# Low part of the weights in two halves on GpSimd, and the per-head sums of squares as two fp32r matmuls

## The reference, cut to what matters

```python
def rmsnorm(x, g):
    x32 = x.astype(jnp.float32)
    y = x32 * lax.rsqrt(jnp.mean(x32 * x32, axis=-1, keepdims=True) + EPS)
    return (y * g.astype(jnp.float32)).astype(x.dtype)

p = h @ w_in[l]
xr, yr, q, k, v, ga, gb = jnp.split(p, cuts, axis=-1)
q = head_rmsnorm(q.reshape(b_, s_, ATT_HEADS, HEAD_DIM), q_norm_g[l])
k = head_rmsnorm(k.reshape(b_, s_, ATT_HEADS, HEAD_DIM), k_norm_g[l])
y_b = stick_breaking_attention(q, k, v)
mix = jax.nn.sigmoid(ga) * y_a + jax.nn.sigmoid(gb) * y_b
x = x + gt1 * (mix @ w_out[l])
```

## Time and profile before

| what | us |
|---|---|
| median of 3 runs (lowest, highest) | 1753.96 (1753.73, 1754.41) |
| time of the profiled execution | 1748.95 |
| its span, first to last instruction | 1747.1 |
| PE busy | 1664.6 (95%) |
| DVE busy | 1020.6 (58%) |
| ACT busy | 789.6 (45%) |
| POOL busy | 711.2 (41%), of which L595 641.7 (532.1 and 109.6) |

### The profile page before, as it was taken

The page is one execution under the profiler, slowest core; times in us unless marked ns, Lnnn a source line. Parts: engine busy times, 40 slices in busy tenths (PEclk is TensorE's granted clock), DMA queues, the critical chain, the costliest instruction groups (busy, mean ns, idle before and its releaser), DMA issues.

```text
span 1747.1 us, 19411 instructions
## 1 busy us (share of the span) xinstructions
PE 1664.6 (95%) x7340; PEld 1346.0 (77%) x7340; DVE 1020.6 (58%) x1156; ACT 789.6 (45%) x986; POOL 711.2 (41%) x325
## 2 busy tenths in 40 slices
PE   3999999999889999999999999999999999999997
PEld 2777787777668878878877888777778877887875
DVE  6676778677637927825632767566437474255642
ACT  2555556565434414523342333676544444244442
POOL 1233333342354444444444543454464151542524
PEclk7999999999899999999999999999999999999999
DMA  9333333332232332233322322211123131331312
GB/s 359 133 109 121 121 123 109 112 106 95 66 96 85 96 95 95 91 118 97 97 73 90 106 90 75 70 41 55 48 85 98 48 109 37 109 97 37 109 48 73
DMA packets 46460, 166.87 MB, mean 96 GB/s; under 512 B 5152, under 2 KB 5280, under 8 KB 45856
## 3 DMA queue, kind: packets, MB, share of 16 engines
q1 hardware_dynamic: 46368, 165.63, 29.1%
HBM read 163.52 MB, written 2.10 MB: 95 GB/s over the span
## 4 chain that ended last, share of the span: by engine, by line
PE 85%; DVE 10%; ACT 2%; issue 1%; DMA 1%; POOL 1%; SPq 0%; DVEq 0%; ACTq 0%
PE lin L621 16%; PE lin L623 16%; PE lin L622 16%; PE big L621 6%; PE big L622 6%; PE big L623 6%; DVE scr L1510 1%; DVE scr L1784 1%; PE m_a L657 1%; PE m_o L740 1%; PE big L720 1%; DVE tmp L2089 1%; DVE y_hi L1793 1%; PE big L731 1%; PE big L733 1%
## 5 line engine op out<-in xcount | busy, mean ns | idle before, releaser
L595 POOL TENSOR_TENSOR w_lo<-raw,w_hi 128x1024 fp32r<-128x1024 f32 (+1 forms) x215 | 532.1, 2480 | 741.3 <-ACT w_hi L1053 740.7
L621 PE MATMUL lin<-h_hi,w_hi 128*128 128x512 f32 x952 | 380.6, 400 | 4.7 <-POOL w_lo L595 3.6
L623 PE MATMUL lin<-h_hi,w_lo 128*128 128x512 f32 x952 | 371.1, 390 | 0.0
L622 PE MATMUL lin<-h_lo,w_hi 128*128 128x512 f32 x952 | 370.8, 389 | 0.0
L1053 ACT ACTIVATE w_hi<-raw 128x1024 fp32r<-128x1024 f32 (+1 forms) x215 | 223.9, 1041 | 160.8 <-PE m_b L639 49.2
L621 PEld LDWEIGHTS lin<-h_hi,w_hi 128*128 128x128 f32 x952 | 179.1, 188 | 46.8 <-POOL w_lo L595 6.6
L622 PEld LDWEIGHTS lin<-h_lo,w_hi 128*128 128x128 f32 x952 | 179.0, 188 | 39.9 <-issue 4.1
L623 PEld LDWEIGHTS lin<-h_hi,w_lo 128*128 128x128 f32 x952 | 178.8, 188 | 37.8
L595 POOL TENSOR_TENSOR qk_hl<-raw,qk_hl 128x1024 fp32r<-128x1024 f32 (+1 forms) x44 | 109.6, 2493 | 159.8 <-ACT qk_hl L1053 159.8
L621 PE MATMUL lin<-y_hi,w_hi 128*128 128x512 f32 x324 | 128.7, 397 | 12.0 <-DVE y_lo L1671 6.9
L622 PE MATMUL lin<-y_lo,w_hi 128*128 128x512 f32 x324 | 127.2, 393 | 0.0
(11 more groups left out here) (440 smaller groups left out, 3199.5 us busy)
## 6 DMA issues: line engine op xcount, KB each, us to landing
raw<-weights SPq DMA_DIRECT2D x245, 512.0 KB, 3.6
slab<-ada SPq DMA_DIRECT2D x32, 512.0 KB, 4.3
scr<-ada SPq DMA_DIRECT2D x16, 512.0 KB, 6.3
raw<-weights SPq DMA_DIRECT2D x10, 256.0 KB, 2.8
x<-x_t SPq DMA_DIRECT2D x2, 1024.0 KB, 6.1
out_t<-scr SPq DMA_DIRECT2D x8, 256.0 KB, 2.1
raw<-weights SPq DMA_DIRECT2D x4, 448.0 KB, 3.4
rgw<-rg_w SPq DMA_DIRECT2D x1, 1024.0 KB, 6.5
```

What stands on the lines that cost most here:

```text
L595: nc.gpsimd.tensor_tensor(lo[:, 0:w], raw[:, s, 0:w], hi[:, 0:w].bitcast(F32), ALU.subtract).then_inc(w_split, 1)
L621: nc.tensor.matmul(psum_of(n), wh, hi(k), start=(k == 0), stop=False)
L622: nc.tensor.matmul(psum_of(n), wh, lo(k), start=False, stop=False)
L623: last = nc.tensor.matmul(psum_of(n), wl, hi(k), start=False, stop=(k == nk - 1))
```

## The change: what it does

**Halves on POOL.** For an entry wider than 512 columns POOL makes the low part in two subtractions, the first of 512 columns, the second of the rest. The first raises a new semaphore `w_half`, which nobody waits for; the second raises `w_split` as before.

**Sums of squares in fp32r.** For the 16 sums of the heads' loop ACT writes the square to `sq_act` as before, then copies it as the high part in fp32r to `sq_hi` (for queries the tile `y_hi[:, 6]`, for keys the tail of `cq_hi`); DVE subtracts it and stores the low part in `sq_lo`; PE multiplies high and low by the full block of ones of `sel_r`, two fp32r matmuls in the place of one in float32. The other sums of squares stay as they were.

```diff
@@ gpsimd, for each entry e
                 pool.wait_ge(w_high, e + 1)
-                nc.gpsimd.tensor_tensor(lo[:, 0:w], raw[:, s, 0:w], hi[:, 0:w].bitcast(F32),
+                if w > 4 * P:
+                    nc.gpsimd.tensor_tensor(lo[:, 0:4 * P], raw[:, s, 0:4 * P], hi[:, 0:4 * P].bitcast(F32),
+                                            ALU.subtract).then_inc(w_half, 1)
+                at = 4 * P if w > 4 * P else 0
+                nc.gpsimd.tensor_tensor(lo[:, at:w], raw[:, s, at:w], hi[:, at:w].bitcast(F32),
                                         ALU.subtract).then_inc(w_split, 1)
@@ tensor
+            def head_square(i, out=m_a[:]):
+                pe.wait_ge(sq_low, i)
+                nc.tensor.matmul(out, sel_r[:, 1], sq_hi[(i - 1) % 2], start=True, stop=False)
+                nc.tensor.matmul(out, sel_r[:, 1], sq_lo[(i - 1) % 2], start=False, stop=True)\
+                    .then_inc(square_used, 1)
...
-                    square(8 + 2 * h + 1, True, True)
+                    head_square(2 * h + 1)
...
-                    square(8 + 2 * h + 2, True, True)
+                    head_square(2 * h + 2)
@@ scalar
+            def head_square(i, src):
+                full = sq_act[:, i % 2]
+                if i > 2:
+                    act.wait_ge(sq_low, i - 2)
+                nc.scalar.activation(full, src, ACT.Square).then_inc(sq_full, 1)
+                act.wait_ge(sq_full, counted(sq_full))
+                if i > 2:
+                    act.wait_ge(square_used, DK + i - 2)
+                nc.scalar.activation(sq_hi[(i - 1) % 2], full, ACT.Copy).then_inc(sq_high, 1)
+                act.wait_ge(sq_high, counted(sq_high))
...
-                    square(9 + 2 * h, A(S1["q"], h))
+                    head_square(2 * h + 1, A(S1["q"], h))
...
-                    square(10 + 2 * h, A(S1["k"], h))
+                    head_square(2 * h + 2, A(S1["k"], h))
@@ vector
+            def square_low(i):
+                dve.wait_ge(sq_high, i)
+                v.tensor_tensor(sq_lo[(i - 1) % 2], sq_act[:, i % 2], sq_hi[(i - 1) % 2].bitcast(F32), SU)\
+                    .then_inc(sq_low, 1)
+                dve.wait_ge(sq_low, counted(sq_low))
             for h in range(HEADS):
                 g = h - 1
+                square_low(2 * h + 1)
                 if g >= 0:
                     dve.wait_ge(z_done, g + 1)
                     dve.wait_ge(ln_done, g + 1)
                     shifted_logs()
+                square_low(2 * h + 2)
                 if h < HEADS:
                     accumulate(ADA_FIRST + 4 * h)
```

More of the change, by code:

```diff
@@ L216, in build @@
         w_high = sem("w_high")
+        w_half = sem("w_half")
         w_split = sem("w_split")
@@ L257, in build @@
         mixed = sem("mixed")
+        sq_full = sem("sq_full")
+        sq_high = sem("sq_high")
+        sq_low = sem("sq_low")
         rooted = sem("rooted")
@@ L486, in build @@
         lm_lo = cq_lo[:].rearrange("p a t -> p (a t)")[:, 0:1280]
+        sq_hi = [y_hi[:, 6], cq_hi[:].rearrange("p a t -> p (a t)")[:, 1280:1280 + T]]
+        sq_lo = [y_lo[:, 6], cq_lo[:].rearrange("p a t -> p (a t)")[:, 1280:1280 + T]]
         block = ctx.enter_context(nc.Block())
@@ L654, in square @@
             def square(count, first, last, out=m_a[:]):
-                pe.wait_ge(squared, count)
+                pe.wait_ge(squared, count if count <= DK else count - 2 * HEADS)
                 nc.tensor.matmul(out, c_("ones"), sq_act[:, count % 2], start=first, stop=last)\
+                    .then_inc(square_used, 1)
[3 more added lines that the diff above has]
+                nc.tensor.matmul(out, sel_r[:, 1], sq_lo[(i - 1) % 2], start=False, stop=True)\
                     .then_inc(square_used, 1)
@@ L772, in _ @@
                 if h == 0:
-                    square(8 + 2, True, True, m_b[:])
+                    head_square(2, m_b[:])
                 elif h < HEADS:
                     pe.wait_ge(rooted, 2 * h + 1)
-                    square(8 + 2 * h + 2, True, True)
+                    head_square(2 * h + 2)
                 if g >= 0:
```

## The result

| what | before | after |
|---|---|---|
| median (lowest, highest), us | 1753.95 (1753.73, 1754.41), 4 runs | 1734.01 (1732.94, 1735.07), 4 runs |
| profiled execution, its span | 1748.95, 1747.1 | 1733.2, 1731.3 |
| mean granted clock of the profiled execution | 0.986 | 0.986 |

The ratio is 0.9886, with a 95% interval of 0.9869 to 0.9903. The change gains 19.9 us by the medians, and 15.75 us by the two profiled executions. The forecast was 8.9 us and 1745.1, with a range that ended at 1740.5. So the direction was right and the size wrong by more than a factor of two.

What follows compares the result with a forecast made beforehand. PE was taken as the bound, busy for 310.00 of 310 us in turns h = 2 to 7. Sums of squares 6.4 us plus halves 2.45 make 8.9; 1753.96 - 8.9 = 1745.1 us, range 1740.5 to 1751.

Steps and rivals of the forecast that it cites:

- part two: Halves on POOL, over the whole run: shorter holds of DVE gain 4.05 us, later entry ends lose 1.6, net 2.45.
- 6.4 + 2.45: Whole run: 6.4 us from the heads' loop's cheaper sums of squares plus 2.45 from the halves on POOL, 8.9 us.
- The first waits for one half and the second for the other, and the sum is as before: Where two held DVE instructions follow each other, each waits for one half, so halving an entry gains nothing.
- the two other waits behind L1795 [...]: nothing: Two PE waits behind a held cast and a plain subtraction: the second half holds the subtraction, so no gain.
- At 430.28 [...] 1.0 us gained: At 430.28 us one DVE block, L1510, is held with PE's modulation behind it; a half gains 1.0 us.
- up to 2 us more where a shifted start lets DVE go first: Upper bound of the halves' gain: DVE starts ahead of POOL and doesn't wait, up to 2 us more.
- The list of places: PE's waits behind DVE's low parts, the modulation block and POOL's low parts: all that the halves can change.
- The slack behind `lm_done`: Heads' loop: a delay of 1 to 2 us from DVE's first new subtraction is covered by 4.6 us.
- the wait of 1.99: PE's wait for `lm_done` in h = 1: 0.40 us less work becomes 0.40 us more waiting, one saving lost.
- I take the same difference off that: The profiled execution stands 5.0 us below the median, before and after alike, so the median becomes 1745.1.
- more than 12, by shifted holds: Case for the whole run: a gain of more than 12 us, by shifted holds; chance 0.03.
- 1751.5: Rival's time if a new PE wait eats all the sums' saving: within 0.4 of no change; within 3.5, chance 0.12.

Runs made afterwards that it cites:

- e1: The kernel before with only the halves on POOL added, sums of squares still in float32: 1743.72 us, ratio 0.9943.
- e2: The kernel before with only the fp32r sums of squares added, POOL's entries whole: 1749.19 us, ratio 0.9974.
- e6: The changed kernel with halves only for entries ahead of w_out, whole entries from there on: 1743.85 us, ratio 0.9948 to the kernel before.
- e7: The changed kernel with whole entries ahead of w_out, halves only from there on: 1740.86 us, ratio 0.9936 to the kernel before.
- e8: The changed kernel with whole entries on POOL and sums from the squares' high part alone, one fp32r matmul: 1744.13 us, ratio 0.9951 to the kernel before.

## Why the prediction was wrong, step by step

The step that failed first is the price of part two, "4.05 - 1.6 = 2.45 us": the halves alone bring 7.0 us at one clock (e1). The second is that the two parts were added as if they didn't touch, 6.4 + 2.45: together they bring 16.0, some 5 more than e1 and e2 apart. The third is the step from the profiled execution to the median, which misses another 4. The mechanism, that POOL's instruction holds DVE's and that a half holds it half as long, was right.

**The sums were right.** Each saves 0.41 us (forecast 0.40 and 0.45). No wait for `sq_low` came, and the two engines' additions in the turns were covered.

**"The first waits for one half and the second for the other, and the sum is as before" was used where it doesn't hold; "the two other waits behind L1795 [...]: nothing" failed at the first of them.** I looked only at the two DVE instructions right ahead of PE. What starts them counts as well. This is the place at 615 us. ACT and DVE there in before:

```profile
609.13 0.63 ACT L1266 ACTIVATE scr<-scr 128x512 f32<-128x512 f32 x1 [1.58 <-DVE scr L1784]
```
```profile
600.66 2.82 DVE L1795 TENSOR_TENSOR y_lo<-tmp,y_hi 128x512 fp32r<-128x512 f32 x1
603.51 2.50 DVE L1757 TENSOR_SCALAR tmp<-tmp 128x512 f32<-128x512 f32 x1
...
607.50 3.10 DVE L1784 SCALAR_TENSOR_TENSOR scr<-big,par,scr 128x511 f32<-128x511 f32 x4
...
611.37 2.45 DVE L1793 CAST y_hi<-tmp 128x512 fp32r<-128x512 f32 x1
```

and after:

```profile
596.98 0.63 ACT L1295 ACTIVATE scr<-scr 128x512 f32<-128x512 f32 x1
```
```profile
594.91 1.53 DVE L1822 SCALAR_TENSOR_TENSOR scr<-big,par,scr 128x511 f32<-128x511 f32 x2
...
599.35 1.40 DVE L1831 CAST y_hi<-tmp 128x512 fp32r<-128x512 f32 x1
600.78 1.63 DVE L1833 TENSOR_TENSOR y_lo<-tmp,y_hi 128x512 fp32r<-128x512 f32 x1
```

The cast and the subtraction do behave as I said: 2.45 and 0.69 became 1.40 and 1.63. But ACT had sat idle for 1.58 us ahead of its Gelu (L1266), until DVE's convolution was done, since two DVE instructions ahead of that (L1795 and L1757 above) had been held for 2.1 us each; with halves the Gelu starts right behind ACT's own work. That is the 1.5 us. The runs bear it out: with whole entries there PE waits 2.9 us at this place (e2, e6), with halves 1.64 (e1, e7 and the change). At the third such wait, 880 us in before, PE's idle time fell only from 1.79 to 1.64 us, as good as forecast.

**"At 430.28 [...] 1.0 us gained" took the hold as halved; in the whole change it went.** POOL and DVE there, after:

```profile
423.31 2.00 POOL L602 TENSOR_TENSOR w_lo<-raw,w_hi 128x512 fp32r<-128x512 f32 x1 [3.64 <-ACT w_hi L1070]
...
422.90 1.29 DVE L1539 SCALAR_TENSOR_TENSOR scr<-slab,par,scr 128x1024 f32<-128x1024 f32 x1
```

In before POOL had begun 0.18 us ahead of DVE (3.25 us); now DVE is 0.4 us ahead of POOL and pays nothing. I had this case in the bounds ("up to 2 us more where a shifted start lets DVE go first"), but as one place's luck. With the halves alone (e1) DVE is still held, for 1.05 us, and PE's wait falls from 3.3 to 2.2, just the 1.0 forecast. The rest is not the shorter piece's doing: e2 has it with whole entries and e8, with PE earlier still, has not. The rows of before don't show which engine will be first once the sums have shifted both.

**The list of places was too short.** The places were drawn from PE's waits that name DVE, POOL or the modulation. DVE's work on the turned queries at 1138 us (L1849) is held too, and PE's idle time behind them was put down to "issue". The chain, DVE and ACT, before, and DVE after:

```profile
1146.02 0.72 issue
1146.74 0.63 PE m_a L915 x4
```
```profile
1138.88 3.37 DVE L1849 TENSOR_TENSOR sq_r<-rstd,sq_r 64x512 fp32r<-64x512 f32 x2 [0.97 <-ACT sq_r L1333]
1142.28 0.69 DVE L1948 TENSOR_TENSOR tmp<-m_o,scr 128x512 f32<-128x512 f32 x1
...
1145.94 0.69 DVE L1959 TENSOR_TENSOR scr_r<-m_a,scr_r 128x512 fp32r<-128x512 f32 x1 [1.16 <-ACT scr_r L1365]
```
```profile
1143.07 0.63 ACT L1340 ACTIVATE y_hi<-tmp 128x512 fp32r<-128x512 f32 x1 [1.68 <-DVE tmp L1948]
...
1145.24 0.60 ACT L1365 ACTIVATE scr_r<-m_a 128x512 fp32r<-128x512 f32 x1
```
```profile
1125.52 2.53 DVE L1887 TENSOR_TENSOR sq_r<-rstd,sq_r 64x512 fp32r<-64x512 f32 x2 [0.98 <-ACT sq_r L1362]
```

The rows give the path: L1948 stands behind the held pair, ACT's L1340 waits 1.68 us for it, ACT's L1365 stands behind L1340 and a table load of 1.28 us, DVE's L1959 waits for L1365 and ends at 1146.63, and PE's transposes, which wait for it by `pt_low`, start at 1146.74. After, the pair takes 0.84 us less and the idle 0.7 us is gone; in e6, where entries are whole there, the pair takes 3.37 and the idle times are 0.73 and 0.72 us again.

**The slack behind `lm_done` was read in the wrong turn.** I took 4.6 us from h = 4, an even turn, in which eight columns of the modulation stand ahead of the suffix sums. In odd turns there are none. Turn h = 3, before, in DVE's timeline and in the chain:

```profile
188.18 1.49 DVE L1612 TENSOR_TENSOR cq_lo<-scr,cq_hi 128x1280 fp32r<-128x1280 f32 x1
```
```profile
192.65 0.23 PE big L731
```

`lm_done` comes at 189.67 (188.18 + 1.49), 3.0 us ahead of PE. With the sums and whole entries it came 4 us later (e2), and PE waited 1.1. The whole change hides the mistake, because halves give those holds back; this is the interaction of the parts, some 5 us, and I had priced them apart. In h = 1 it was the same: I had forecast that the wait of 1.99 grows by the 0.40 us saved, and it fell to 0.7.

**"I take the same difference off that" was wrong.** The 5.0 us between the profiled execution of before and its median are a matter of its granted clock, 0.986 and 0.981, and the kernel after doesn't share it. That alone is 4 of the 11 us by which I missed. Why its runs stand at 0.985 and 0.986 is open. Fewer waits alone don't do it: e8, without the waits for `lm_done`, stands at 0.981.

**What was right:** 2.1 for 2.0 at 472, 1.1 for 1.05 at 748, 0.5 for 0.7 at each of the two waits for `w_split`, and that the two engines take turns within an entry. In the list of cases the right one is "more than 12, by shifted holds", which had 0.03 of the chance; it deserved more, since the halves touch every held instruction and I had followed a handful. One slip in the rivals changed nothing: 1751.5 is 2.5 us from no change, not 0.4.

## What to carry to other kernels

Where two engines share a port, cut the operation of the one that isn't the bound, and where its end is awaited, leave it whole: the piece sets what the other engine pays, the whole entry's end what PE pays. Follow each chain back over ACT to the engine's next start before saying that a shorter hold brings nothing, and ask of an idle time marked "issue" what else ended just ahead of it. Take slack from the tightest turn of a loop, price the parts of a change together, look for half-speed stretches before putting a loss down to a wait, and compare a profiled execution with a median only at the same granted clock.

## What the runs showed of the hardware

**The hold goes with the piece, less a constant.** The cast's median over its plain 426 ns, and POOL's mean for the piece under which it stands:

| columns of a piece | POOL, ns | cast held, ns |
|---|---|---|
| 1024 | 2530 | 2066 |
| 512 | 1422 | 971 |
| 256 | 850 | 420 |
| 128 | 555 | 142 |

The hold is POOL's time less 0.41 to 0.46 us in each row. By the differences between these rows POOL pays some 0.26 to 0.29 us a piece whatever its length (an estimate), so a cut pays until that makes the entry late. The Trainium skill (SBUF — State Buffer, Who interferes with whom) says that whoever starts first keeps the port for the whole instruction; the runs agree, and add that DVE gets it at the end of a piece, even if POOL's next one is ready: in none of the four kernels is any of the 24 casts held for longer than one piece (2509, 1401, 849 and 572 ns at most).

**The clock doesn't follow from the waits alone.** Windows of 8 us behind the wait for `lm_done` in h = 1 (the clock is the last but two, PE's matmuls stand in the first brackets), in before and in e2:

```profile
92.00:100.00 8.00, 7.85 (x40) 6.55 (x41) 7.72 (x9) 1.83 (x3) 0.00 (x0) 1.00 0.69 247
```
```profile
92.00:100.00 8.00, 7.83 (x35) 7.15 (x36) 7.72 (x9) 1.32 (x2) 0.00 (x0) 0.79 0.59 205
```

PE had waited 1.99 us in the one and 1.94 in the other, some 8 us behind a first wait for POOL of 1.22 and 1.6, and only e2 was granted part of the time at 1.2 GHz in place of 2.4, which cost it 1.5 us. What decides between them no run here shows.
